# An RWKV-7 chunk scan on one core: products in the diagonal quadrants, the inverse turned by VectorE, and the order of the steps

## The reference

```python
def rwkv_scan(r, decay, k, v, kk, a, s0):
    def step(s, inp):
        rt, wt, kt, vt, kkt, at = inp
        sa = jnp.einsum('bhvk,bhk->bhv', s, -kkt)
        s = s * wt[:, :, None, :] + sa[..., None] * (kkt * at)[:, :, None, :] + vt[..., None] * kt[:, :, None, :]
        return s, jnp.einsum('bhvk,bhk->bhv', s, rt)
    s, y = lax.scan(step, s0, tuple(jnp.moveaxis(t, 1, 0) for t in (r, decay, k, v, kk, a)))
    return jnp.moveaxis(y, 0, 1), s
```

## Time and profile before

| | us |
|---|---|
| runs (three), median | 3032.43 |
| lowest, highest | 3031.48, 3041.18 |
| profiled execution, its own time | 3034.87 |
| profiled execution, span of the core | 3032.8 |
| TensorE busy with matmuls | 2637.6 (87%) |
| TensorE weight loads (beside the matmuls) | 1842.2 (61%) |
| VectorE busy | 667.8 (22%) |
| ScalarE busy | 449.2 (15%) |
| GpSimd busy | 46.8 (2%) |
| mean granted TensorE clock | 0.942 |

### The profile page before, as it was taken

How to read it: one execution, slowest core, us unless ns; L and a number is a source line. 1 busy time by engine, 2 the same in 40 slices (tenths; PEclk the granted TensorE clock), 3 DMA queues, 4 the chain that set the end, 5 groups by cost and what they waited for, 6 DMA issues and landing times.

```text
span 3032.8 us, 74281 instructions
## 1 busy us (share of the span) xinstructions
PE 2637.6 (87%) x34271; PEld 1842.2 (61%) x34272; DVE 667.8 (22%) x1096; ACT 449.2 (15%) x809; POOL 46.8 (2%) x147
## 2 busy tenths in 40 slices
PE   6998788999998776669766769999999999999993
PEld 2653533444443655557665559696969696877872
DVE  1132513000001375534555621000000000000001
ACT  3231112000001333241222120000000000000001
POOL 0000004000000000000000000000000000000000
PEclk9998898999999889989999879999999999999996
DMA  6216017222223200032000227887979788888870
GB/s 226 80 59 249 1 56 275 81 76 77 72 81 121 74 2 4 4 123 82 3 5 4 66 98 254 330 297 290 344 282 346 280 319 302 319 306 314 306 290 14
DMA packets 178948, 493.73 MB, mean 163 GB/s; under 512 B 9362, under 2 KB 73188, under 8 KB 172500
## 3 DMA queue, kind: packets, MB, share of 16 engines
q1 hardware_dynamic: 176852, 482.73, 44.6%
q0 software_dynamic: 1792, 6.19, 0.7%
HBM read 487.84 MB, written 1.05 MB: 161 GB/s over the span
## 4 chain that ended last, share of the span: by engine, by line
PE 82%; DVE 7%; issue 7%; ACT 2%; DMA 1%; SPq 0%; POOL 0%; DVEq 0%; ACTq 0%; POOLq 0%
PE banks L982 23%; PE banks L998 13%; PE banks L586 10%; PE banks L718 10%; PE banks L794 8%; PE banks L728 5%; PE banks L628 2%; PE banks L525 1%; PE banks L955 1%; DVE rstd L1295 1%; PE banks L967 1%; PE banks L913 1%; PE banks L680 1%; DVE ring_arena L1597 1%; PE banks L751 1%
## 5 line engine op out<-in xcount | busy, mean ns | idle before, releaser
L982 PE MATMUL banks<-ring_arena 128*64 128x112 f32 x14336 | 694.0, 259 | 0.0
L982 PEld LDWEIGHTS banks<-ring_arena 128*64 128x64 f32 x14336 | 687.1, 137 | 8.8 <-issue 8.0
L794 PE MATMUL banks<-ring_arena 64*64 64x64 f32 x13824 | 265.9, 225 | 152.0 <-issue 115.8
L998 PE MATMUL banks<-ring_arena 128*112 128x512 f32 x896 | 385.8, 592 | 0.0
L794 PEld LDWEIGHTS banks<-ring_arena 64*64 64x64 f32 x13824 | 242.0, 139 | 173.3 <-issue 146.7
L586 PE MATMUL banks<-ring_arena 128*128 128x256 f32 (+1 forms) x1024 | 315.4, 471 | 21.7 <-ACT ring_arena L1042 12.7
L718 PE MATMUL banks<-ring_arena 128*128 128x512 f32 x704 | 305.3, 597 | 0.0
L998 PEld LDWEIGHTS banks<-ring_arena 128*112 128x112 f32 x896 | 158.0, 177 | 221.9 <-issue 221.9
L586 PEld LDWEIGHTS banks<-ring_arena 128*128 128x128 f32 x1024 | 199.9, 196 | 137.7 <-issue 96.5
L1756 DVE TENSOR_TENSOR ring_arena<-ring_arena,banks 128x448 f32<-128x448 f32 x32 | 19.9, 621 | 1034.0 <-PE banks L982 1034.0
L718 PEld LDWEIGHTS banks<-ring_arena 128*128 128x128 f32 x704 | 134.8, 192 | 169.8 <-issue 169.8
(11 more groups left out here) (264 smaller groups left out, 1620.5 us busy)
## 6 DMA issues: line engine op xcount, KB each, us to landing
ring_arena<-in_moe_w_gu SPq DMA_DIRECT2D x256, 896.0 KB, 5.5
ring_arena<-in_moe_w_d SPq DMA_DIRECT2D x112, 1024.0 KB, 6.9
ring_arena<-in_mod_w SPq DMA_DIRECT2D x48, 1024.0 KB, 7.1
ring_arena<-in_ff_w_gu SPq DMA_DIRECT2D x22, 1024.0 KB, 5.1
ring_arena<-in_rw_w_rkv SPq DMA_DIRECT2D x20, 1024.0 KB, 10.4
ring_arena<-in_gla_w_in SPq DMA_DIRECT2D x12, 1024.0 KB, 5.4
ring_arena<-in_ff_w_d SPq DMA_DIRECT2D x11, 1024.0 KB, 4.9
ring_arena<-in_gla_w_out SPq DMA_DIRECT2D x4, 1024.0 KB, 13.7
```

What stands on the lines that cost most here:

```text
L794: ins = T.matmul(bank[rows[o], col:col + CH], lhs[rows[r], p, :], EYE2[rows[r], :] if rhs is None else rhs[rows[r], p, :], start=start, st ...
L982: ins = T.matmul(bank[CH * h:CH * h + CH, (c % 4) * CAP:(c % 4) * CAP + CAP], w[:, kk, c * P + CH * h:c * P + CH * h + CH], XG[:, 2 * kp + ...
L998: ins = T.matmul(ps[6 + h][0:CAP, :], HX[:, 2 * u + k, :], w[:, k, 512 * h:512 * h + 512], start=(u == 0 and k == 0), stop=(u == WD_UNITS ...
```

## The change

- All products of the scan stand in the two diagonal quadrants: `heads` runs over the pairs p and the two halves r and reads and writes the same half. `swapped`, `home` and `home_and_swapped` are gone. One step's results fill one bank; each direction has four banks.
- The removal product is computed once per chunk (B times A, bank 0) in `removal_product`, for the next chunk, between SA and U of this one. ScalarE copies it to NT (`removal_out`); VectorE (`base`) masks it into TT, adds the identity, and turns TT to T.
- T is turned to TT at each of the levels 1 to 4 by VectorE's transpose of 32 x 32 blocks (`turn`), in place of a product with the identity and a ScalarE copy.
- The turned values are kept in four tiles `V_TOK`, one for each chunk of tokens. Direction 0 turns chunks 0 and 1 and direction 1 turns chunks 3 and 2, in the first two chunks of a segment; the later chunks read what the other direction has turned.
- Products that don't depend on the running level are placed between X and TX of the levels: Lak (and Mrb) at level 1, (Mrk and) Bt at level 2, Kt and the value turn at level 3, W at level 4, none at level 5.
- VectorE's `sums`, `removal` and `front` of the next chunk stand after the mask of X at levels 3, 4 and 5, ahead of the add to T. U comes before y on TensorE.

The core of the diff:

```diff
-            PE_STEPS.append(["NT", "Vt", "N", "Lak"] + ["Mrb", "Mrk"] * lat + ["Bt", "TT0", "X1", "TX1", "Kt"]
-                            + [x for l in range(1, 4) for x in (f"TT{l}", f"X{l + 1}", f"TX{l + 1}")]
-                            + ["TT4", "X5", "TXT5", "W high", "W", "SA"] + ["y high", "y"] * lat + ["U"])
-            AC_STEPS.append(["NT", "Vt", "TT0", "Bt"] + ["Kt"] + ["TT1", "TT2", "TT3", "TT4", "W", "SA"])
+            PE_STEPS.append(["X1", "Lak"] + ["Mrb"] * lat + ["TX1", "X2"] + ["Mrk"] * lat + ["Bt", "TX2", "X3", "Kt", "TX3",
+                             "X4", "W", "TX4", "X5", "TXT5", "SA", "U"] + ["y"] * lat)
+            AC_STEPS.append(["Bt", "Kt", "W", "SA"])
...
+            def heads(d, b, lhs, rhs, first=True, last=True):
+                for p in range(HP):
+                    for r in rows:
+                        ins = T.matmul(ps[4 * d + b][r, p * CH:p * CH + CH], lhs[r, p, :],
+                                       EYE2[r, :] if rhs is None else rhs[r, p, :],
+                                       start=first and p == 0, stop=last, skip_group_check=True)
+                return ins
+
+            def removal_product(g):
+                for d in range(2):
+                    w = WORK[d]
+                    pe.wait_ge(pre_v[d], 3 * g + 3)
+                    pe.wait_ge(fr_s[d], FRS.value(g // SC, g % SC, "B"))
+                    heads(d, 0, w["B"], w[f"A{g % 2}"]).then_inc(nt_pe[d], 1)
...
+                x_step(1)
                 for d in both:
...
+                    step(d, 1, [(w[d]["K"], A[d])], [(FRS, "K")])
...
+                tx_step(1)
+                x_step(2)
...
+                    step(d, 2, [(w[d]["B"], None)], [(DVS, "Mrb")] if lat else [])
+                tx_step(2)
+                x_step(3)
                 for d in both:
+                    step(d, 1, [(w[d]["K"], None)], [(DVS, "Mrk")] if lat else [(DVS, "Lak")])
+                if i < 2:
                     for d in both:
+                        pe.wait_ge(ac_s[d], ACS.value(lat, i, "Bt"))
+                        heads(d, 2, VT[:, i if d == 0 else SC - 1 - i], None).then_inc(S["vt"], 1)
+                tx_step(3)
+                x_step(4)
...
+                    step(d, 1, [(w[d]["Lak"], V[d]), (A[d], w[d]["ST"])], [(ACS, "Kt"), (DVS, "Lak")])
+                tx_step(4)
+                x_step(5)
                 for d in both:
+                    step(d, 3, [(w[d]["X"], w[d]["TT"])], [(DVS, "X5"), (DVS, "TT4")])
                 for d in both:
+                    step(d, 2, [(w[d]["TT"], w[d]["W"])], [(ACS, "W"), (DVS, "TT5")])
+                if i < SC - 1:
+                    removal_product(g + 1)
+                for d in both:
+                    step(d, 3, [(w[d]["Kt"], V[d]), (w[d]["Bt"], w[d]["SA"])], [(ACS, "SA")])
                     if lat:
+                        step(d, 1, [(w[d]["ST"], R[d]), (V[d], w[d]["Mrk"]), (w[d]["SA"], w[d]["Mrb"])], [])
...
+            def base(g):
+                for n in range(3):
+                    for d in range(2):
+                        w = WORK[d]
+                        if n == 0:
+                            dve.wait_ge(nt_pe[d], g + 1)
+                            ins = Vv.tensor_tensor(w["TT"], scan_bank(d, 0), over(LM[0][d]), ALU.mult)
+                        else:
+                            dve.wait_ge(t0_dve[d], 3 * g + n)
+                        if n == 1:
+                            ins = Vv.tensor_tensor(w["TT"], w["TT"], over(EYE2), ALU.add)
+                        if n == 2:
+                            ins = Vv.transpose(flat2(w["T"]), flat2(w["TT"]))
+                        ins.then_inc(t0_dve[d], 1)
...
+                def turn(d):
+                    need(d)
+                    Vv.transpose(flat2(w[d]["TT"]), flat2(w[d]["T"])).then_inc(dv_s[d], 1)
+                    said_one(d)
...
                 for l in range(1, 6):
                     for d in range(2):
+                        mult(d, w[d]["X"], scan_bank(d, 0), over(LM[l][1 - d]), (PES, f"X{l}"))
...
+                    if l == 3 and i < SC - 1:
+                        sums(g + 1)
+                    if l == 4 and i < SC - 1:
+                        removal(g + 1)
+                    if l == 5 and i < SC - 1:
+                        front(g + 1)
                     for d in range(2):
+                        t = w[d]["T" if l < 5 else "TT"]
+                        add(d, t, t, scan_bank(d, 3), (PES, f"TX{l}" if l < 5 else "TXT5"))
+                    if l < 5:
+                        for d in range(2):
+                            turn(d)
                 if i < SC - 1:
+                    base(g + 1)
```

More of the change, by code:

```diff
@@ L782, in scan, with step @@
                 both = range(2)
-                rows = [slice(0, CH), slice(CH, P)]
-                def wait_for(d, need):
+                g = SC * lat + i
+                def step(d, b, terms, need):
                     for c, n in need:
                         pe.wait_ge(c.sems[d], c.value(lat, i, n))
[L789 to L827, removed]
+                    for q, (lhs, rhs) in enumerate(terms):
+                        ins = heads(d, b, lhs, rhs, q == 0, q == len(terms) - 1)
@@ L1211, in scan @@
                 for d in range(2):
[L1212 to L1220 removed]
+                    step(d, w[d]["Kt"], 1, 1.0, [(PES, "Kt")])
@@ new lines, in scan @@
+                if i < 2:
+                    for d in range(2):
+                        act.wait_ge(S["vt"], 4 * lat + 2 * i + d + 1)
+                        C.activation(V_TOK[i if d == 0 else SC - 1 - i], scan_bank(d, 2), ACT.Copy).then_inc(S["vt_out"], 1)
+                if i < SC - 1:
+                    for exp in (exp1, exp3, exp2):
+                        for d in range(2):
+                            exp(d, g + 1)
+                for d in range(2):
+                    step(d, w[d]["W"], 1, -1.0, [(PES, "W")])
@@ L1221, in scan @@
                 for d in range(2):
-                    step(d, w[d]["W"], scan_bank(d, 0, 0), -1.0, [(PES, "W")])
-                for d in range(2):
-                    step(d, w[d]["SA"], scan_bank(d, 1, 0), 1.0, [(PES, "SA")])
+                    step(d, w[d]["SA"], 2, 1.0, [(PES, "SA")])
+                if i < SC - 1:
+                    removal_out(g + 1)
             for sg in range(2):
@@ L1603, in add @@
                     said_one(d)
-                for d in range(2):
-                    t = by_bank(w[d]["T"])
-                    mult(d, t, scan_bank(d, 1, 0), over(LM[0][1 - d]), (PES, "Lak"))
-                    mult(d, by_bank(w[d]["Lak"]), scan_bank(d, 1, 1), over(STRICT[d]))
-                    add(d, t, t, over(EYE2))
-                if lat:
-                    for d in range(2):
-                        mult(d, by_bank(w[d]["Mrb"]), scan_bank(d, 0, 0), over(INCL[d]), (PES, "Mrk"))
-                        mult(d, by_bank(w[d]["Mrk"]), scan_bank(d, 0, 1), over(INCL[d]))
@@ L1659, in _ @@
                 front(SC * sg)
+                base(SC * sg)
                 if sg:
```

127 lines of the change are left out of this document (59 added, 68 removed).

## The result

The changed kernel takes 2984.06 us (median of four, 2982.42 to 2988.62), the kernel before 3036.55 (four runs now, 3031.48 to 3041.18). The ratio is 0.983, 95% interval 0.9806 to 0.9854. The forecast was 2988, faster. In the profiled executions the span went from 3032.8 to 2980.7 us, 52.1 less; 48.7 of it lies in the two scans, the other 3.4 where nothing was changed.

What follows compares the result with a forecast made beforehand. The scans were held to be bound by the arrival of TensorE's instructions; afterwards rows 332, levels 33, starts 11 and uneven fetch 6 give 382 us against 426.3, so the kernel takes 2988 us, range 2955 to 3024.

Steps and rivals of the forecast that it cites:

- The bound before: In the old scans, TensorE's instructions arrive at 3.74 us per block of 256; 114 blocks make 426.3 us.
- The rows: Both scans after the change: 11264 weight loads with their matmuls, 88 blocks, 29.5 ns each in diagonal quadrants, 332 us.
- Between levels: TensorE's new waits for VectorE between dependent steps of a chunk: 15 us in context, 18 in latent, 33 in all.
- The wait after T's add: At each of four levels x waits for the add to T, 0.23 us idle, 0.9 us a chunk.
- The starts: Start of each segment: base delays X1, 7.6 us idle for both, plus 1.7 us each for low clock; 11 us.
- The transposes: VectorE's turns of T to TT, taken at 0.69 us each, the row for a multiply over the same elements.
- Rival 3: Slower: VectorE's transposes, up to 2.74 us each, come out from under the gap products; kernel 3088 us; chance 0.06.
- The uneven fetch: Instruction blocks arriving every 3.5 to 4.0 us around TensorE's 3.78 add some 0.1 on about 60 blocks, 6 us.
- rival 1: The instruction stream alone decides and diagonal rows keep up: scans 340 us, 86 less, kernel 2946; chance 0.08.
- rival 2: The granted clock drops after idle at level 5, 2 us twice per chunk, 32 us, kernel 3020; chance 0.12.
- rival 4: Slower: "issue" stays 1.75 us after each block whatever the block takes; scans 487 us, kernel 3093; chance 0.04.
- The sum: Both scans together 382 us against 426.3, 44 less; kernel 2988 us for a median.

## Why the prediction was right, point by point

- *The bound before* was read rightly: the arrival of TensorE's instructions. The run with the value turn five times shows it, as idle and all the time rose by more than the added work.
- *The rows*: 11264 and 88 blocks, as counted. A row was put at 29.5 ns; measured are 64 loads in 1.94 us and 128 in 3.83, 29 ns each, after 0.13 for the last. 332 us became 329.
- *Between levels*, 33 us forecast, some 25 measured (21.9 as waits behind adds and masks, the rest too short to be listed). The wait after T's add was over-priced: 0.23 us a level was forecast, and the 128 loads over TX4 and X5 take 3.89 us, where 128 from 1495.24 on, two terms without such a wait, take 3.83: under 0.1. I had added the last matmul's time and the 0.22 after it; the first of the two overlaps the end of the step (VectorE starts 1.20 after TX starts, not 1.36). Over eight chunks that is some 5 us. Level 5's mask was put at 0.86, measured 0.64 by the matmuls and 0.78 by the weight loads. SA's wait for front was put at 2.0 and 3.2, measured 1.8 and 3.0; sums in chunk 2 at 1.6, measured 1.5.
- *The starts*, 11 us forecast. The idle before X1 is 2.6 us in each scan (3.8 forecast), since the first 64 loads take 3.52 and 3.69 us instead of 1.9, at the lower clock. X1 starts 6.3 and 6.5 us after the first product (5.1 and 6.3 forecast), which makes 9 us beyond its 1.9 of work. What the forecast missed is that the lower clock lasts past X1: by the stretches above it cost another 4 to 5 us there (half of 3.1 and of 6.0).
- *The transposes* were put at 0.69 us, measured 0.686. Rival 3 priced them at up to 2.74; it fell.
- *The uneven fetch*, 6 us forecast, was nothing: 0.4 us of "issue". This term was mis-sized. The mean of 3.74 us per block that I set beside TensorE's 3.78 held 19 us of waits for VectorE and ScalarE in the old scans; a block costs 3.4 at the margin. So TensorE's pace, 3.74 measured, had room, and rival 1 was wrong the same way: the diagonal rows, not the stream, set the pace, as the old order in the diagonal quadrants has them, without "issue".
- *Clock* (rival 2): 0.98 and 0.96 in the two scans. The loss that it names did come, though hardly: once in the eight chunks, after a wait for front, 2.8 us at the lower level, 1.4 us lost, where it had two in each chunk and 32 us. A second execution of the changed kernel has two such stretches in the latent scan.
- *Gaps that stay* (rival 4): "issue" went to 0.4 us. Its 1.75 us was the longer kind of gap; over the old scans the mean was 1.2 (119.6 us in 101 waits). It is also not the case of a hidden fetch, for which the prediction let it stand: that one, in which more or fewer instructions change nothing, fell with the run with the value turn five times.
- *The end of a scan* has no term in the forecast: 1.5 and 2.3 us go from TensorE's last product to VectorE's last step.
- *The sum*: 382 us forecast for the scans (170 and 212), 377.6 measured (166.7 and 210.9). It is closer than its terms. Rows, levels and fetch were some 17 us too high, and the clock after X1 and after front (6) and the ends of the scans (4) were not in it; with the starts 2 us below their 11, what I can name comes to 373, and 4 to 5 us are not accounted for. For the whole kernel, 2988 forecast and 2984 measured is closer still, by luck: the gain was put at 44 us and came to 52, of which 3 lie outside the scans, while the median of the kernel before, which I had from three runs (3032.4), is 4 us higher over four.
- *The shares*: the forecast did not say how its parts share. Each taken away alone, the transposes are 38.6 us and the order 38.9, against 15 us that the quadrants cost on the old order. These do not add up to the 48.7 of the whole, since each fills waits that another leaves.

## What to carry to other kernels

When an engine that no other engine holds up shows even bursts with "issue" between them, count the instructions of a burst against the packets of the instruction queue. If they match, count instructions, not work: what only makes the work slower (here fewer quadrants) is nearly free up to the fetch's pace (15 us lost for 151 us of added work). Once that limit is gone, each chain between engines shows whole, so place independent products in the gaps of the chain, at the last level too, and put preparation for later behind the step that the other engine waits for. Price a limit by its margin (add or remove some of it), not by its mean, which carries other waits. And before a stretch is priced by the instruction, read the granted clock in it.

## What the runs showed of the hardware that was not expected

In the two diagonal quadrants a row with one moving column cost as much as a row with 64: 29 ns at full clock (62 loads in 1.89 us) and 53 ns at the lower level (62 in 3.43 us), against 29 and 53 (114 in 6.0 us). So the 32 one-column products bought no cheap instructions, and while they ran the granted clock fell to the lower level in most places (0.90 and 0.91 over the scans, 0.99 and 0.97 without them); why was not tried. A fetched block of 256 TensorE instructions costs 3.4 us at the margin. And a scan's start, after 9 us without work, runs at the lower level: 64 rows in 3.52 us where 29.2 ns a row would be 1.87, and in the latent scan 114 rows more in 6.0 us.
